# Five lent buffers of a weight stream hold loaded weights in place of their rounded first halves

## The reference, cut to what matters

```
mod = silu(c) @ w_mod[l] + b_mod[l];  shift, scale, gate = split(mod)
h = rmsnorm(x) * (1 + scale) + shift
q_a, k_a, v_a, g_a, q_i, k_i, w_i, q_b, k_b, v_b, g_b = split(h @ w_in[l])
y_a = sparse_attention(top-64 of the index scores of q_i, k_i, w_i) * silu(g_a)
y_b = groupnorm(retention(rotary(q_b), rotary(k_b), v_b)) * silu(g_b)
x = x + gate * (concat(y_a, y_b) @ w_out[l])
```

## Time and profile before

| | |
|---|---|
| median of three runs | 2072.11 us (2061.25 to 2075.68) |
| the profiled execution | 2069.3 us |
| its span | 2067.5 us |
| PE busy / DVE busy / ACT busy | 1919.1 / 1713.3 / 1246.5 us |
| load engines' share | 77% |
| mean granted clock of PE | 0.949 of full speed |

### The profile page before, as it was taken

How to read it: one execution, slowest core, us unless ns; L and a number is a source line. 1 busy time by engine, 2 the same in 40 slices (tenths; PEclk the granted TensorE clock), 3 DMA queues, 4 the chain that set the end, 5 groups by cost and what they waited for, 6 DMA issues and landing times. The chain is left out here.

```text
span 2067.5 us, 34027 instructions
## 1 busy us (share of the span) xinstructions
PE 1919.1 (93%) x13292; PEld 1784.4 (86%) x13292; DVE 1713.3 (83%) x2198; ACT 1246.5 (60%) x1927; POOL 280.2 (14%) x182
## 2 busy tenths in 40 slices
PE   5999989999999988999999997999989879999898
PEld 5789889999998888899989976998888769988887
DVE  6886978877998898888998887789879876898776
ACT  5566644744666656555666667456766574566573
POOL 0000031041110012311000100222101002222010
PEclk9998999999999989999999998899999889999999
DMA  7686666767999776788889876768779867686785
GB/s 240 206 286 204 214 226 212 258 217 265 311 354 355 232 264 211 259 294 299 295 303 337 291 277 209 242 201 290 242 245 326 302 196 247 204 277 223 268 300 204
DMA packets 270764, 536.88 MB, mean 260 GB/s; under 512 B 31880, under 2 KB 40973, under 8 KB 269581
## 3 DMA queue, kind: packets, MB, share of 16 engines
q1 hardware_dynamic: 270317, 532.62, 77.0%
q10 hardware_dynamic: 288, 2.10, 0.3%
HBM read 532.55 MB, written 2.10 MB: 259 GB/s over the span
## 5 line engine op out<-in xcount | busy, mean ns | idle before, releaser
L150 PE MATMUL ps<-hh_r,w 128*128 128x256 f32 x3384 | 860.9, 294 | 47.2 <-DVE ring_r L1832 27.4
L150 PEld LDWEIGHTS ps<-hh_r,w 128*128 128x128 f32 x3384 | 669.4, 198 | 61.0 <-DVE ring_r L1832 35.0
L150 PE MATMUL ps<-hlo,ring_r 128*128 128x256 f32 x2856 | 715.8, 289 | 0.0
L1832 DVE SCALAR_TENSOR_TENSOR ring_r<-ring,w 128x1024 fp32r<-128x1024 f32 (+1 forms) x455 | 568.2, 1263 | 158.2 <-ACT w L1381 156.3
L1381 ACT ACTIVATE w<-ring 128x1024 fp32r<-128x1024 f32 (+1 forms) x455 | 470.9, 1051 | 215.1 <-PE ps L150 85.7
L150 PEld LDWEIGHTS ps<-hlo,ring_r 128*128 128x128 f32 x2856 | 567.0, 199 | 1.1 <-issue 0.7
L150 PE MATMUL ps<-hlo,AR_r 128*128 128x256 f32 x1064 | 260.3, 284 | 0.0
L1832 DVE SCALAR_TENSOR_TENSOR AR_r<-AR,w 128x1024 fp32r<-128x1024 f32 x167 | 211.0, 1275 | 46.2 <-ACT w L1381 45.2
L150 PE MATMUL ps<-w,AR_r 128*128 128x512 f32 x584 | 236.1, 404 | 7.1 <-DVE AR_r L1832 7.1
L1381 ACT ACTIVATE w<-AR 128x1024 fp32r<-128x1024 f32 x167 | 173.8, 1055 | 67.3 <-PE ps L150 25.4
L150 PEld LDWEIGHTS ps<-hlo,AR_r 128*128 128x128 f32 x1064 | 206.8, 194 | 0.6 <-issue 0.5
(11 more groups left out here) (212 smaller groups left out, 2724.0 us busy)
## 6 DMA issues: line engine op xcount, KB each, us to landing
ring<-in_w_in SPq DMA_DIRECT2D x294, 512.0 KB, 4.9
ring<-in_w_mod SPq DMA_DIRECT2D x124, 512.0 KB, 5.5
ring<-in_w_up SPq DMA_DIRECT2D x113, 512.0 KB, 5.5
AR<-in_w_in SPq DMA_DIRECT2D x75, 512.0 KB, 5.2
ring<-in_w_out SPq DMA_DIRECT2D x65, 512.0 KB, 5.9
AR<-in_w_up SPq DMA_DIRECT2D x63, 512.0 KB, 5.7
ring<-in_w_down SPq DMA_DIRECT2D x62, 512.0 KB, 5.7
AR<-in_w_mod SPq DMA_DIRECT2D x56, 512.0 KB, 5.6
```

Of the source, the lines that this page charges most:

```text
L150: return e.matmul(o, l, x, start=start, stop=stop, skip_group_check=True)
L1832: return e.scalar_tensor_tensor(o, a, s, b, op0, op1)
```

## The change

Five calls of `lend_ar` name "raw" where they named "w1". Nothing else is different: the chunks, their order, the arithmetic and the stretches of the arena are the same. The first-half places are then the five of `w1`, and six once B2 is lent; the landing places are two more in the first half of each layer, one more in the rest. A raw place needs a semaphore for its landing; `lend` takes one of those that are there.

```
             if L == 0:
                 lend_ar("W0", 11008, "raw", b_qi[0], before)
                 lend_ar("V0", 8960, "raw", b_vb[0], before)
-                lend_ar("V1", 9984, "w1", b_vb[0], before)
+                lend_ar("V1", 9984, "raw", b_vb[0], before)
             lend_ar(f"QB0{L}", 4864, "raw", b_rot[L][0], before)
-            lend_ar(f"QB1{L}", 5888, "w1", b_rot[L][1], before)
+            lend_ar(f"QB1{L}", 5888, "raw", b_rot[L][1], before)
...
         def lend_retain():
             over = (ret_pe, ("sv", L, 3))
             lend_ar(f"V{2 * L + 2}", 8960, "raw", b_last if L else b_vb[1], over)
-            lend_ar(f"V{2 * L + 3}", 9984, "w1", b_last if L else b_vb[1], over)
+            lend_ar(f"V{2 * L + 3}", 9984, "raw", b_last if L else b_vb[1], over)
```

## The result

The changed kernel takes 2075.88 us (median of 20 runs, 2070.05 to 2086.35), the kernel before 2068.81 (20 runs, 2060.24 to 2076.25). The ratio of after to before is 1.0043, with a 95% interval of 1.003 to 1.0056: slower by some 8.9 us (2068.8 x 0.0043). The ratio is that of the means; the medians are 7.1 us apart. The profiled execution of after took 2071.63 us, its span is 2069.8, the mean granted clock 0.951.

What follows compares the result with a forecast made beforehand. PE was taken as the bound, with DVE and the load queue close; 8.4 + 4.0 + 1.9 + 1.0 + 3.4 - 1.5 = 17.2 us on the profiled 2069.3 gave 2086.5, stated as 2087 us, range 2068 to 2104.

Steps and rivals of the forecast that it cites:

- the clock: One half-rate stretch charged at each of the two top-k stretches: 3.4 us, between 0 and 10.2.
- the later half of layer 0: In w_out, one split less ahead but one landing place more: +1.0 us, between -3 and +5.
- what gets better: PE's waits for DVE's other work, 1.7 us, shrink as that work comes earlier: 1.5 us back, between 0 and 4.
- Top-k stretch: Both layers: second halves ready two DVE slots later at the last qn chunk, 4.2 us each, 8.4 us together.
- Sparse attention: After the top-k, PE waits for later second halves: 2.0 us a layer, 4.0 in all, between 0 and 6.4.
- Start of layer 1: During the norm three chunks are ready instead of four, so PE's wait begins one chunk earlier: 1.9 us.
- (a): Rival: PE lacks landing, so two more landing places shorten waits for second halves: 2055, likelier 2062; chance 0.11.
- (b): Rival: top-k to sparse attention, DVE's backlog swallows the lost lead: +4 us, 2073; chance 0.19.
- Its premise: DVE's backlog bounds top-k through sparse attention, where PE waits anyway, 21.4 us without a visible releaser.
- (c): Rival: every wait pulls the clock down and layer 0's later half costs in full: 30.4 us, 2100; chance 0.22.
- its own sign: PE's wait in a top-k stretch comes in one piece of over 2 us, not spread over four chunks.

Runs made afterwards that it cites:

- the runs with the short top-k: Kernel before and changed kernel, each with top-k rounds on 8 columns (selection not the reference's): ratios to the kernel before 1.0005 and 1.001.
- `v3_and_v5`: Against the kernel before, V5 holds raw weights, V3 too up to layer 0's third w_out product, then first halves again: 0.9967, 2061.56 us.
- the repeat: The kernel before, unchanged, run under another name for a second profile: ratio 1.0000 (0.9976 to 1.0024), 8 runs.
- V5 alone: Against the kernel before, only V5 turned from first-half place into landing place: ratio 0.998 (0.9963 to 0.9997), 2063.43 us.
- without the places: Against the changed kernel, the five stretches lent to nobody, so no landing place more: ratio to the kernel before 1.0035, 2077.34 us.
- the two halves of the change: Against the kernel before, only V1, QB10 and QB11 turned into landing places: 1.0027; only V3 and V5 turned: 0.9984.
- nine places: Against the kernel before, V0, QB00 and QB01 also hold first halves: ratio 1.0055; with V5 as landing place on top, 1.0034.

## Why the prediction was right and where it failed

The sign was right, and the top-k as the largest cost; the size was not, 17.2 us forecast and 8.9 measured. Three terms of the sum failed: the clock (+3.4, where the time at half rate didn't change), the later half of layer 0 (+1.0, measured -2.5), and what gets better (-1.5, measured -3.5 at one glu alone, and 9.1 us less of waits for anything but second halves over the block). Term by term, the sizes by the pieces of the one pair of executions, the causes by the runs.

*Top-k stretch, +8.4.* Right. +4.4 and +3.9 us, three waits in each, and the runs with the short top-k show the cause: without the length of the rounds both pieces are equal. The way to read it off the trace was sound: the second half two slots later on DVE's own timeline, against PE's begin.

*Sparse attention, +4.0.* Its size was near, and by luck. +3.2 and +2.4 us, but 3.4 us at half rate in layer 0 and 6.8 in layer 1 lie in them, which cost 1.7 and 3.4. The waits account for the small rest: PE's rows there sum to 2.1 before and 3.5 after in layer 0, and to 4.6 and 4.2 in layer 1.

*Start of layer 1, +1.9.* Right: the wait is 7.88 in place of 5.88 and comes after 48 matmuls in place of 64, the piece +2.4. `v3_and_v5`, which keeps the sixth place there, has 35.37 as before.

*The clock, +3.4.* This step failed. The second block spent 112.6 us at half rate before and 112.6 after, not counting a stretch that the end of the program cuts (2.9 and 3.1 us). The top-k waits brought no such stretch (clock 1.00 before and after, 0.90 and 0.91), the sparse attention brought 10.2 us at half rate, and w_out of layer 0 and the third glu of layer 1 lost 16.5; the rest lies in the pieces not shown and in the long wait at the start of layer 1. In the repeated runs the mean granted clock was 0.9499 over 20 runs of after and 0.9492 over 93 of before, where two stretches of 3.4 us would have shown as 0.0016 less. I had read the clock as a price on top of each new wait. A wait that goes can give one back, and not each has one: of PE's waits of 1.8 to 4 us outside the starts of the layers, 7 of 9 before and 6 of 11 after had a stretch at half rate begin in them or within 1.5 us behind them. The six top-k waits, of 0.9 to 1.3 us, had none.

*Later half of layer 0, +1.0.* Failed in sign: -2.5. The five kernels of the study with five places here and the changed one took 91.2 to 92.3 us, the seven with six places and the kernel before 92.1 to 98.4, mean 94.1. PE's waits grow, 7.4 to 10.0 us, as I said; but at half rate it is 1.7 us in place of 14.8, and a wait for `macc` in w_out is gone (1.1 us before, 2.7 in the repeat). That it is the stretches that matter here is read, not shown by an experiment: four kernels with six places happened to have fewer of them and took 92.1 to 92.7.

*What gets better, -1.5.* Failed in size, and this is the one to learn from. V5 alone is worth 0.002, some 4 us. I looked for waits on DVE's other work, saw the 1.7 us row, and missed the row of `macc` with 3.2 us in the same view; and I priced the wait alone, not the half-rate stretch behind it (the third glu: 1.9 us less wait and 3.4 us less at half rate, which is 1.7, against 3.5 us in all). The 1.7 us did go, inside the sparse attention of layer 0, and so did 2.7 us of waits for `stg` and for ACT that I hadn't looked at.

So 17.2, less 3.4 for the clock, 3.5 for w_out, 2.0 for what gets better and 0.1 for the top-k, and 1.6 and 0.5 more for the sparse attention and the start, makes 10.3 us; with 0.2 for the pieces not shown this is the 10.5 of the profiled pair, and the repeated runs have 8.9. The level was off too: 2072.11 was the median of three runs, 3.3 us above that of twenty, as large as any small term; and 2087 had added the sum to the profiled execution, where the median would have given 2089.

The rivals. (a) Landing is not what PE lacks: 0.0035 without the places, 0.0043 with them. The advice to double-buffer so that loads overlap with compute, which the Trainium skill gives (Trainium Kernel Development and Optimization, Best Practices), brought no time in this kernel, which has many landing places already: the waits for loads more than halved, 95.3 to 39.9 us, and the kernel was slower. (b) The lead isn't swallowed: the 8.3 us of the top-k stay lost, though its time, 2073, is nearer to the result than mine; the give-back came from elsewhere, w_out and the glu. Its premise was misread, too: of the 21.4 us without a visible releaser only 1.4 stand in the two pieces of the sparse attention, the rest behind them, and 19.7 us are left after the change. (c) Every wait pulling the clock down is refuted by the equal 112.6 us, and its own sign, a top-k wait in one piece of over 2 us, didn't come (0.95, 1.33 and 1.34). In the sparse attention alone it had a point: the 2.0 us wait of either layer was followed by half rate. The Trainium skill (TensorE: Matmul & The Clock Gate, Part 1) has activity set the rate; that agrees with where the stretches stand, but their sum doesn't follow the sum of PE's waits, 69.4 to 79.3 us here.

Open: why the two halves of the change add up to less than the whole, 0.0011 against 0.0043; how much of the loss with nine places is the order and how much the landing places taken away; whether V3 as a landing place gains anything; and how much of the gain in w_out is a stretch of the clock that another small shift would move as well.

## What to carry to other kernels

In engine lists that are strictly in order, the number of buffers a stage may run ahead is also the priority of that stage over all other work. Here seven beat five where a long job of DVE stood between the splits, nine (with fewer landing places) cost as much as five, and six beat seven where the other work was what PE waited for. So set it stage by stage, and when a lead is given up, price both sides from the same view of waits: those for the split that will grow, and those for the other work that will go. A wait for a landing only counts if the engine that stands in it is itself waited for.

## What the chip showed that I had not expected

Half-rate stretches of 3.4 us move about among the waits rather than add to them: 13.1 us less at half rate in the later half of layer 0, though PE waited 2.6 us more there. The wait at the start of layer 1 grew by 2.0 us to 7.88, its piece by 2.4: next to nothing beyond the wait itself. And the runs of one and the same kernel spread by 16 us (2060.24 to 2076.25), nearly twice the effect, so that a difference of 0.4% took 20 runs a side.
